# Where VectorE places the out projection's last copies in the entry of the first MLP

## The reference, cut to what matters

```python
mix = jnp.concatenate([y_pool, y_sb], axis=-1) @ w_out[i]
h = h + rms_norm(mix, g_mix_post[i])
m = rms_norm(h, g_mlp_pre[i]) @ w_up[i]
m = jnp.square(jax.nn.relu(m)) @ w_down[i]
h = h + rms_norm(m, g_mlp_post[i])
```

## Time and profile before

| | |
|---|---|
| median of 3 runs | 2991.03 us (2988.72 to 2991.25) |
| the profiled execution's own time | 2994.82 us |
| its span, first to last instruction | 2993.0 us |
| granted TensorE clock, mean over the span | 0.994 of full |
| TensorE (PE) busy | 2931.6 us, 98% |
| VectorE (DVE) busy | 1522.2 us, 51% |
| ScalarE (ACT) busy | 791.8 us, 26% |
| GpSimd (POOL) busy | 882.3 us, 29% |

### The profile page before, as it was taken

The page is one execution under the profiler, slowest core; times in us unless marked ns, Lnnn a source line. Parts: engine busy times, 40 slices in busy tenths (PEclk is TensorE's granted clock), DMA queues, the critical chain, the costliest instruction groups (busy, mean ns, idle before and its releaser), DMA issues.

```text
span 2993.0 us, 33566 instructions
## 1 busy us (share of the span) xinstructions
PE 2931.6 (98%) x13246; PEld 2330.7 (78%) x13246; DVE 1522.2 (51%) x1566; ACT 791.8 (26%) x1066; POOL 882.3 (29%) x467
## 2 busy tenths in 40 slices
PE   8999999999999999999999999999999999999998
PEld 6876677788888888678888866777887888888886
DVE  3649945444455455893332265555536333433356
ACT  2148943312122221341012133333113111111112
POOL 2330022233333333243333321300342333333331
PEclk9999999999999999999999999999999999999999
DMA  3121032122222221221314344331411111111111
GB/s 119 50 71 29 1 127 85 43 78 98 98 98 98 90 96 67 100 107 53 116 71 137 115 97 127 93 71 71 169 49 36 49 44 49 49 49 49 49 49 70
DMA packets 85013, 233.05 MB, mean 78 GB/s; under 512 B 19312, under 2 KB 27760, under 8 KB 84144
## 3 DMA queue, kind: packets, MB, share of 16 engines
q1 hardware_dynamic: 79616, 211.49, 21.5%
q10 hardware_dynamic: 5296, 20.19, 1.7%
HBM read 176.26 MB, written 28.05 MB: 68 GB/s over the span
## 4 chain that ended last, share of the span: by engine, by line
PE 88%; DVE 7%; issue 2%; ACT 1%; POOL 0%; DVEq 0%; ACTq 0%; POOLq 0%
PE ps L410 59%; PE ps L465 4%; PE ps L2509 3%; PE ps L2482 3%; PE ps L3152 3%; PE ps L1313 3%; PE ps L2523 2%; PE ps L2182 1%; PE ps L838 1%; DVE stick_sp L1057 1%; PE ps L2904 1%; DVE stick_sp_hi L1068 1%; DVE stick_a L1081 1%; PE ps L437 1%; PE ps L3204 1%
## 5 line engine op out<-in xcount | busy, mean ns | idle before, releaser
L317 POOL TENSOR_SCALAR w_hi<-w_raw 128x1024 fp32r<-128x1024 f32 x186 | 199.7, 1074 | 1651.0 <-PE ps L410 1078.9
L319 POOL TENSOR_TENSOR w_lo<-w_raw,w_hi 128x1024 fp32r<-128x1024 f32 x186 | 499.1, 2683 | 15.5
L410 PE MATMUL ps<-x_hi,w_hi 128*128 128x512 f32 x1104 | 341.3, 390 | 0.7 <-POOL w_lo L740 0.6
L410 PE MATMUL ps<-x_lo,w_hi 128*128 128x512 f32 x1104 | 340.1, 389 | 0.0
L410 PE MATMUL ps<-x_hi,w_lo 128*128 128x512 f32 x1104 | 339.8, 389 | 0.0
L410 PE MATMUL ps<-hidden_hi,w_lo 128*128 128x512 f32 x800 | 246.3, 389 | 0.0
L410 PE MATMUL ps<-hidden_hi,w_hi 128*128 128x512 f32 x800 | 246.3, 389 | 0.0
L410 PE MATMUL ps<-hidden_lo,w_hi 128*128 128x512 f32 x800 | 246.3, 389 | 0.0
L410 PEld LDWEIGHTS ps<-x_hi,w_hi 128*128 128x128 f32 x1104 | 206.7, 188 | 45.3 <-issue 1.6
L410 PEld LDWEIGHTS ps<-x_lo,w_hi 128*128 128x128 f32 x1104 | 207.2, 188 | 43.3
L410 PEld LDWEIGHTS ps<-x_hi,w_lo 128*128 128x128 f32 x1104 | 207.2, 188 | 43.2
(11 more groups left out here) (452 smaller groups left out, 5147.8 us busy)
## 6 DMA issues: line engine op xcount, KB each, us to landing
w_raw<-wall SPq DMA_DIRECT2D x213, 512.0 KB, 3.2
ada_raw<-wada SPq DMA_DIRECT2D x48, 512.0 KB, 4.1
gates_scratch<-gate_out ACTq DMA_DIRECT2D x16, 512.0 KB, 2.6
gate_in<-gates_scratch SPq DMA_DIRECT2D x8, 1024.0 KB, 7.3
residual<-x_t SPq DMA_DIRECT2D x8, 512.0 KB, 7.6
residual<-x_t SPq DMA_DIRECT2D x2, 2048.0 KB, 9.7
emb_scratch<-emb_out ACTq DMA_DIRECT2D x8, 512.0 KB, 2.6
embedding<-emb_scratch SPq DMA_DIRECT2D x4, 1024.0 KB, 6.3
```

The lines of the kernel that those rows point to most:

```text
L317: nc.gpsimd.tensor_scalar(w_hi[:, slot, :], w_raw[:, slot, :], 1.0, 1.0, ALU.mult, ALU.mult).then_inc(w_split, 1)
L319: nc.gpsimd.tensor_tensor(w_lo[:, slot, :], w_raw[:, slot, :], w_hi[:, slot, :].bitcast(F32), ALU.subtract).then_inc(w_split, 1)
L410: last = nc.tensor.matmul(ps[:, banks + c, :], lhs, x[:, k0 + k, c * HALF:(c + 1) * HALF], start=k == 0 and n == 0, stop=k == nk - 1 and n ...
```

## The change

It moves four things, and adds or removes no instruction of the arithmetic.

- On VectorE the first `mix_half` call goes from step 2 to step 5 of the first half, and the second from step 4 to step 7.
- On VectorE the low part of the weight block goes from step 5 to step 6.
- On TensorE `stat_1` goes from behind step 2 to behind step 6.
- On ScalarE the Ln and Exp of the second factor go from the middle of the first half's squares (k = 5) to behind the last of them.

```diff
-            if k == 5:
-                act.wait_ge(*stat_full.at(0))
-                act_half_rstd(act, 1, 3)
             entry_square(k, 0)
             if k == 1:
                 ring_high(act, GM + 2, GM + 1)
+        act.wait_ge(*stat_full.at(0))
+        act_half_rstd(act, 1, 3)
         for k in range(8):
...
-        steps[0, 2] = stat_1
+        steps[0, 6] = stat_1
...
         def between(k, c):
-            if (k, c) == (2, 0):
+            if (k, c) == (5, 0):
                 mix_half(dve, 0, 1, -1, -2)
-            if (k, c) == (4, 0):
+            if (k, c) == (7, 0):
                 mix_half(dve, 1, 1, 2, -1)
             if k >= 3 and k % 2:
                 add_entry(k - 3, c)
-            if (k, c) == (5, 0):
+            if (k, c) == (6, 0):
```

## The result

| | before | changed |
|---|---|---|
| median of 12 runs each | 2989.66 us (2986.68 to 2996.12) | 2996.72 us (2994.88 to 3001.48) |
| ratio to before, 95% interval | | 1.0022 (1.0014 to 1.0030) |
| the profiled execution's own time | 2994.82 us | 3001.48 us |
| span | 2993.0 us | 2999.7 us |
| mean granted clock | 0.994 | 0.994 |

The change costs about 7 us by the medians, 4 to 9 us by the interval. The forecast was +4.0 us and 2995.0 us, with a range up to 2998.5 us. The sign and the range held; the sum was too small. The forecast started from a median of three runs, 2991.0 us, and twelve runs of the kernel before have 2989.66 us.

What follows compares the result with a forecast made beforehand. TensorE, carrying 88% of the chain, was taken as the bound, with 4.4 us idle in the entry. Three terms taken as +3.0 us plus +1.0 us for the clock, on 2991.0 us, gave 2995.0 us, range 2990.5 to 2998.5 us.

Steps and rivals of the forecast that it cites:

- Term 1: First half of the MLP entry, up to VectorE's low part of tile 5: exchanged waits make it +0.5 us later.
- Term 2: Start of the entry's second half: the second factor comes later and VectorE stands idle, +5.1 us.
- Term 3: Second half of the entry: a vanished 1.53 us wait and part of a stretched sum give back 2.4 us.
- Term 4: First steps of the entry: TensorE's clock falls to half behind 4.3 us idle, +1.0 us (0.5 to 1.8).
- The second fall: Rival: the clock falls again where TensorE has no slack, +6.6 us in all, 2997.6 us; chance 0.12.
- The 0.11 for a change of over 6 us: Chance given to the whole kernel getting slower by over 6 us.
- The signs that the text named: Entry trace: first matmul near 506.5 us, 0.7 us VectorE waits, second half from 524.8 us, clock below 1, end near 554.5 us.
- the delay is made up later: Rival: a later stage that waits for a transfer or another engine takes the 4 us, 2991 us; chance 0.07.
- The clock stays up: Rival: no fall of TensorE's clock in the entry, +3.0 us, 2994.0 us; chance 0.16.

Runs made afterwards that it cites:

- the run of the first wait: Changed kernel, but TensorE's first block waits for the first copy only ahead of the second half; entry length 61.1 us, ratio 1.0020.
- the split later: Changed kernel, but ScalarE makes the third weight block's high part behind the last square, so GpSimd's split runs later; entry length 59.0 us, ratio 1.0012.
- all four couplings cut: Changed kernel with first wait only where the bank is needed, squares waiting for own sums, factor behind step 4, weight split later; 54.2 us entry, ratio 0.9996.

## Why the prediction was right, and where its sum was short

**Term 1 (+0.5 us up to the low part of tile 5): right.** The first matmul came 11.07 us into the entry (508.41 - 497.34) where the text said 506.5 us, 11.0 us in. The two waits ahead of the sums were there, 0.70 us each. The run that took TensorE's late start away gave back the 1.6 us that the half clock had cost and nothing more: the idle time costs nothing by itself.

**Term 2 (+5.1 us for the factor): right.** The factor alone gave +5.16 us, VectorE's idle time was 5.07 us where the text said 5.6 us, and with the factor at step 4 it vanished with 3.8 us of the length. The 5.6 us were a slip that the sum does not use: the text let VectorE end its first half at 519.2 us as in the kernel before, though its own low part of tile 5 is 0.5 us later, which gives 519.7 us and 5.1 us of idle time.

**Term 3 (-2.4 us given back): the step that failed.** The first half of it held: the wait of 1.53 us for a high part is gone. The second did not: "It comes again, but meets a later part of VectorE's sequence, with something like 1.3 us left of it: -0.9 us". The stretched operation was 2.89 us long after (2.87 us before), and 2.87 to 2.90 us in every trace that has the split at this place, whether a sum or a scaling stood there. GpSimd's split begins a little ahead of it each time and takes 2.5 to 2.75 us. Nothing of it came back. From the start of the second half to TensorE's step 5 it took 538.11 - 519.15 = 18.96 us before and 545.69 - 528.37 = 17.32 us after, so the term is -1.6 us where the text had -2.4 us. With terms 1 and 2 as the run of the first wait shows them without the cost of the first fall, 29.43 - 23.68 = +5.75 us, the sum of terms 1 to 3 is +4.1 us instead of +3.2 us (the text took 3.0). The execution with the shorter fall bears that out: 60.1 us less its exposed 0.5 us is 59.5 us, +4.2 us. The text knew "between 0 and -2.2" and took a middle value that no row gave; the end at 0 was right.

**Term 4 (+1.0 us, between 0.5 and 1.8, for the first fall): right in kind and size.** It was 1.54 us in one execution and 0.53 us in the other, and it worked through the wait named: the high part of tile 4 behind the odd square of tile 1, for which ScalarE was held 4.04 us and 3.03 us. The second fall was a rival with a chance of 0.12, a price of up to 2.6 us and +6.6 us in all. It came in three of the five traces that have TensorE's wait of 2.0 us ahead of step 5 of the second half, not in the two of the change itself. Each time it cost 1.6 us. Its chance was set too low. That "the pieces are as short as those that did no harm before" was a reading of one execution, and the same short pieces were followed by a fall in another. And the piece that the late falls followed was 2.0 us long where the text had 1.3 us, because term 3 gave nothing back. The 0.11 for a change of over 6 us does not follow from its words either, since half of 0.12 is 0.06.

The signs that the text named came, some of them later than it said. In the change's first trace, shifted by the 1.87 us that its entry starts later, the low part of tile 5 ended at 518.9 us and the second half began at 526.5 us, a little past the ranges given (518.5 and 526.4 us), and the end of the entry came 5.7 us later where the text had some 4 us.

So the change costs 4.2 us and, by how the clock falls, 0.5 to 1.5 us more, and where the late fall comes 1.6 us on top: 4.7 to 7.3 us. The medians' +7 us lie at the upper end of that, and their interval of 4 to 9 us takes all of it in. Whether late falls were common in the timed runs of the change stays open. A timed run has only the mean granted clock of its whole span: on average 0.9932 in 21 runs of the change and 0.9936 in ten with the split later. And the ratios of the change and of the split later, 1.0022 and 1.0012, lie 3.0 us apart, where the traces of the two, neither with a late fall, lie 2.0 us apart. Both point to late falls in a part of the change's runs, and neither shows them, since the differences are hardly larger than their noise.

Of the other rivals, "the delay is made up later" is out by the medians, which would be equal: the interval of the ratio starts at +4 us. Single spans can't settle it. Of the 6.7 us between the two spans 1.9 us lay ahead of the entry, where both programs are the same, and 5.7 us in it, which leaves -0.9 us behind it; but that last part differs by 5.1 us between the two traces of the kernel before alone (2442.2 and 2437.1 us). "The clock stays up" did not happen in either of the two traces of the change. Without the first wait alone the long idle time is broken up and the clock still fell; of all variants of the changed kernel only the one with all four couplings cut kept it at 1.00.

## What to carry to other kernels

When a producer's small tasks are pushed back, look at what is counted by them, not only at what reads their output: here a bank that was not yet needed, two squares of other tiles, and a norm's factor hung on them. Cutting these three couplings, and moving the weight split away, turned +5.7 us into -1.2 us, of which the split is worth 0.6 us in the kernel before. When the late engine changes from one to another, a cost that was covered (a stretched operation beside GpSimd's, a fall of the clock) becomes exposed, so each cover has to be looked up again for the new order. A term for which no row gives a value belongs in the sum at the end that costs more, or at least in both sums.

## What the runs showed of the hardware

- **The clock can fall behind short idle times, and not in every execution.** The kernel before had 1.00 in one trace and 0.51 and 0.64 in the next, with the same idle times of 0.79 and 1.31 us; the wait of 2.0 us in the second half was followed by a fall in three traces of five, and one of 1.94 us in the first half (all four couplings cut) by none. A fall came behind 4.36 us of idle time in every trace that has it, six of six. It lasted 6.8 us in four of them and 3.4 us in two; the falls behind shorter idle times in these entries all lasted 3.4 us.
- **The price of a fall is set by who is late behind it.** The same fall was free in the kernel before (55.34 us against 55.36 us without it), 0.5 to 1.5 us in the first half of the two traces of the change, and 1.6 us, nearly the half of its 3.4 us, late in the second half.
- **A VectorE operation that starts just behind GpSimd's tensor-tensor is held for its whole length.** A sum or a scaling, which take 0.68 to 0.75 us elsewhere, was listed at 2.87 to 2.90 us in each trace with the split beside it. After the change GpSimd's ran from 540.68 to 543.22 us, and the scaling that began at 540.88 us ended at 543.77 us. The Trainium skill (SBUF — State Buffer, Who interferes with whom) says that a VectorE instruction with two inputs in SBUF contends with a GpSimd instruction that reads SBUF. Of VectorE's two-port modes it says that whoever issues first gets the shared ports for the whole instruction. These traces agree with the first, and look like the second for operations with two inputs: the price was 2.2 us in each of the nine traces where the split met such an operation, and the middle value of term 3 had no row for it.
